# First expert's rows by TensorE products instead of a gather, and spare products before and after the expert loops

## What is computed

```python
def hier_moe(x, ...):                       # x is rms_norm(x, norm_ffn)
    # router: best of 4 groups, then the best two of its 8 experts
    ...
    # every expert e, on the rows routed to it:
    hid = jax.nn.silu(xb @ w_gate[e]) * (xb @ w_up[e])     # 1024 -> 512
    return hid @ w_down[e]                                 # 512 -> 1024
    # weighted, and added to the token's row
```

## Time and profile before

| | |
|---|---|
| median of 3 runs | 1993.37 us (1992.31 to 1996.8) |
| the profiled execution | 1999.4 us, its span 1997.7 us |
| TensorE busy | 86% of the span, mean granted clock 0.906 of full speed |
| VectorE, ScalarE, GpSimd busy | 29%, 20%, 12% |
| DMA, share of 16 engines over the span | 57.9% (SyncE's queue), 8.3% (GpSimd's) |
| expert stage of layer 0, rank products to last down product | 612.5 to 1140.8 us |
| expert stage of layer 1 begins | 1442.6 us |

### The profile page before, as it was taken

How to read it: one execution, slowest core, us unless ns; L and a number is a source line. 1 busy time by engine, 2 the same in 40 slices (tenths; PEclk the granted TensorE clock), 3 DMA queues, 4 the chain that set the end, 5 groups by cost and what they waited for, 6 DMA issues and landing times.

```text
span 1997.7 us, 28368 instructions
## 1 busy us (share of the span) xinstructions
PE 1720.3 (86%) x9488; PEld 906.5 (45%) x9489; DVE 575.2 (29%) x1537; ACT 406.3 (20%) x866; POOL 249.2 (12%) x350
## 2 busy tenths in 40 slices
PE   6798998888994889889998789999778898988985
PEld 4455565555452444444443344456434444444332
DVE  2234343333233111111111165663411111111113
ACT  2122223323111111111111123432111111111112
POOL 1132001332001111111111120000011111111110
PEclk9899889989995899998998889997879989999988
DMA  4343103645246999999999770030399999999983
GB/s 146 79 137 96 47 4 109 209 159 172 83 160 271 393 409 405 410 409 408 402 411 405 302 287 1 17 129 1 134 378 410 416 413 410 407 406 404 401 356 142
DMA packets 83610, 516.31 MB, mean 258 GB/s; under 512 B 22746, under 2 KB 41131, under 8 KB 57067
## 3 DMA queue, kind: packets, MB, share of 16 engines
q1 hardware_dynamic: 61962, 461.35, 57.9%
q0 software_dynamic: 21568, 53.93, 8.3%
HBM read 508.03 MB, written 26.52 MB: 268 GB/s over the span
## 4 chain that ended last, share of the span: by engine, by line
PE 70%; DMA 12%; issue 8%; DVE 5%; ACT 3%; SPq 1%; DVEq 1%; ACTq 0%; POOLq 0%; POOL 0%
PE ps L1866 61%; PE ps L1871 9%; DMA mem<-in_moe_w_up 6%; DMA mem<-in_cache_mla 2%; DMA mem<-moe_rows_back 1%; DVE mem L1525 1%; DMA mem<-moe_rows_in,mem 1%; DMA mem<-in_x_sample 1%; SPq L441 1%; ACT mem L936 1%; ACT mem L724 0%; DVE mem L1644 0%; DMA moe_rows_back<-mem 0%; DVE mem L1570 0%; DVE mem L1249 0%
## 5 line engine op out<-in xcount | busy, mean ns | idle before, releaser
L1866 PE MATMUL ps<-mem 128*64 128x512 f32 (+16 forms) x7352 | 1450.7, 494 | 119.7 <-issue 48.6
L1866 PEld LDWEIGHTS ps<-mem 128*64 128x64 f32 (+4 forms) x7352 | 653.3, 153 | 830.7 <-issue 731.5
L1871 PE MATMUL ps<-mem 128*128 128x128 f32 (+3 forms) x2136 | 309.6, 287 | 150.3 <-DVE mem L1525 45.7
L724 ACT ACTIVATE mem<-ps 128x512 f32<-128x512 f32 (+4 forms) x364 | 195.8, 551 | 900.1 <-PE ps L1866 543.9
L1871 PEld LDWEIGHTS ps<-mem 128*128 128x128 f32 (+3 forms) x2136 | 260.1, 169 | 252.0 <-issue 189.4
L1525 DVE TENSOR_TENSOR mem<-mem,ps 64x512 f32<-64x512 f32 x64 | 44.2, 690 | 470.8 <-ACT mem L936 470.8
L653 POOL DMA_INDIRECT mem<-moe_rows_in,mem x70 | 65.3, 933 | 561.4 <-issue 537.6
L1536 DVE COPY mem<-ps 64x512 f32<-64x512 f32 x64 | 44.4, 693 | 313.5 <-PE ps L1866 313.5
L663 POOL DMA_INDIRECT moe_rows_back<-mem x64 | 59.0, 922 | 356.0 <-DVE mem L1536 348.9
L936 ACT ACT_TABLE_LOAD x32 | 41.1, 1283 | 219.5 <-PE ps L1866 219.5
L936 ACT ACTIVATE mem<-ps 64x512 f32<-64x512 f32 x64 | 37.6, 588 | 199.6 <-PE ps L1866 199.2
(11 more groups left out here) (221 smaller groups left out, 501.0 us busy)
## 6 DMA issues: line engine op xcount, KB each, us to landing
mem<-in_moe_w_gate SPq DMA_DIRECT2D x64, 2048.0 KB
mem<-in_moe_w_up SPq DMA_DIRECT2D x64, 2048.0 KB
mem<-in_moe_w_down SPq DMA_DIRECT2D x64, 2048.0 KB, 21.1
mem<-in_cache_mla POOLq DMA_DIRECT2D x160, 160.0 KB, 4.0
mem<-in_cache_mla SPq DMA_DIRECT2D x96, 160.0 KB, 5.0
mem<-moe_rows_back SPq DMA_DIRECT2D x8, 1024.0 KB, 8.9
mem<-in_mla_wo SPq DMA_DIRECT2D x1, 4096.0 KB, 13.2
moe_rows_in<-mem POOLq DMA_DIRECT2D x8, 512.0 KB, 3.5
```

What stands on the lines that cost most here:

```text
L724: return act.activation(out, in_, ACT.Copy)
L1866: return pe.matmul(out, lhsT, rhs, start=start, stop=stop)
L1871: return pe.transpose(out, in_, ident[at:at + n, at:at + n])
```

## The change

The first expert's rows are no longer gathered. VectorE multiplies expert 0's marks with `rstd` into `direct` (128 x 5 x 64), TensorE computes the transposed rows as x (stationary, 128x128) times `direct` (moving, 64 columns), 8 column groups of x by 5 tiles, and VectorE copies them out of PSUM times the norm's gain, in place of ScalarE's `rows_T(0, 0)`. These 40 products go in three pieces between `numbers(1, 1)`, `pre_mm`, `listrow_mm` and `numbers(2, 0)`. GpSimd gathers from expert 1 on, and the two gathers ahead of the loop no longer wait for a transpose. SyncE issues expert 1's gate and up before its wait for the stored rows; only down waits for them, and expert 2's loads wait for `sel_ready` in layer 1 alone. TensorE also runs `keep_busy`: products of the identity with 512 columns of constants, whose result nobody reads, 20 of them in each layer between the last `logits` and the wait for `sel_ready`, and 24 between the end of layer 0's experts and `hidden(0)`.

```diff
-INTO = ((FETCHES + 1) // 2, FETCHES // 2)
+INTO = ((FETCHES + 1) // 2 - 1, FETCHES // 2)
...
+        direct = mem[:, router.at:router.at + TILES * BLK].rearrange("p (t r) -> p t r", t=TILES)
...
@@ SyncE, experts(L)
+                gate_up(1, 0)
                 for b in range(2):
                     sp.wait_ge(sig[f"xn_out{b}"], landed(f"xn_out{b}", SAVES[b] * (L + 1)))
-                gate_up(1, 0)
                 down(1, 0)
-                sp.wait_ge(sig["sel_ready"], happened("sel_ready", L + 1))
                 if L:
+                    sp.wait_ge(sig["sel_ready"], happened("sel_ready", L + 1))
                     sp.wait_ge(sig["state_out"], landed("state_out", 2))
                 gate_up(2, 1)
@@ GpSimd
-                    g.wait_ge(sig["xt_mm"], happened("xt_mm", (NE + 1) * L + q - 1))
-                    turnstile(g)
+                    if not isinstance(q, int) or q > 2:
+                        g.wait_ge(sig["xt_mm"], happened("xt_mm", (NE + 1) * L + q - 1))
+                        turnstile(g)
...
-                for q in range(LOOK):
+                for q in range(1, LOOK):
                     fetch(q, q % 2)
@@ ScalarE
-                rows_T(0, 0)
@@ VectorE
                     mark(q, q % 2)
-                    if q:
+                    if q == 0:
+                        v.drain()
+                        v.tensor_tensor(direct, onehot[0], rstd[:, 0:TILES].unsqueeze(2).broadcast_to([P, TILES, BLK]), ALU.mult
+                                        ).then_inc(sig["direct_ready"], 1)
+                    else:
                         numbers(q - 1, (q - 1) % 2)
...
+                v.wait_ge(sig["xt_mm"], happened("xt_mm", (NE + 1) * L + 1))
+                v.tensor_tensor(xeT[0], ps[:, 5, :].rearrange("p (k t) -> p k t", k=KD),
+                                gainT_ffn[:, L].unsqueeze(2).broadcast_to([P, KD, BLK]), ALU.mult).then_inc(sig["xeT_ready"], 1)
                 numbers(LOOK - 1, (LOOK - 1) % 2)
@@ TensorE
+            def keep_busy(n):
+
+                for _ in range(n):
+                    mm(ps[:, 7, :], ident, mem[:, TILES * D:TILES * D + FF], True, True)
+
             def experts(L):
...
+                pe.wait_ge(sig["lg_ready"], happened("lg_ready", TILES * L + PT))
+                keep_busy(20)
                 pe.wait_ge(sig["sel_ready"], happened("sel_ready", L + 1))
...
+                def first_rows(k0, k1):
+
+                    for k in range(k0, k1):
+                        for T in range(TILES):
+                            last = mm(ps[:, 5, k * BLK:(k + 1) * BLK], x[:, T * D + k:(T + 1) * D:KD], direct[:, T, :],
+                                      T == 0, T == TILES - 1)
+                    if k1 == KD:
+                        last.then_inc(sig["xt_mm"], 1)
...
                 numbers(1, 1)
+                pe.wait_ge(sig["direct_ready"], happened("direct_ready", L + 1))
+                first_rows(0, 3)
 
                 pe.wait_ge(sig["nb_ready"], happened("nb_ready", L + 1))
                 mm(...).then_inc(sig["pre_mm"], 1)
+                first_rows(3, 6)
                 pe.wait_ge(sig["list_ready"], happened("list_ready", L + 1))
...
+                first_rows(6, KD)
                 pe.wait_ge(sig["lst_ready"], happened("lst_ready", L + 1))
-                fetched_T(0, 0, even + 1)
                 numbers(2, 0)
...
             experts(0)
+            keep_busy(24)
```

More of the change, by code:

```diff
@@ L101 @@
     "sum_mm": ("s_mm", UNITS + 23),
+    "direct_ready": ("a_ms", TILES),
     "third_pages0": ("w_a_in", 1),
@@ L2229, in expert @@
                     last.then_inc(sig["gu_mm"], 1)
-                    fetched_T(e + 1, 1 - b, (odd if b == 0 else even + 1) + pair + 1)
+                    fetched_T(e + 1, 1 - b, (odd if b == 0 else even) + pair + 1)
                     numbers(e + LOOK, 1 - b)
```

## The result

The changed kernel takes 2022.94 us in the median of 3 runs (2018.4 to 2028.85) against 1993.37 us: a ratio of 1.0147, with a 95% interval of 1.010 to 1.0193. It is slower by 1.5%, some 29 us. The forecast was slower by 13.0 us, and its range ended at 2014 us. The profiled execution lasted 2018.4 us, with a span of 2016.7.

The account below looks back on a forecast made before the run. Work ahead of the end of expert 0's gate and up was taken to set each layer's end; +1.8, +4.0 and +7.2 made +13.0 us, from 1993.4 to 2006.4 us, range 1996 to 2014.

Parts of the forecast that it names:

- What bounds the kernel: Expert loops: products and weight loads start from expert 0's gate and up; each microsecond ahead comes out at layer end.
- absorbed by transfers: Rival in the expert loops: if loads set the end, waits swallow the delays and 0 to 4 us remain; chance 0.04.
- The price of a spare product: Ahead of rank products: 0.43 us a record, 17.2 us per 20, plus 1.7 for a clock fall; gaps too short.
- The rival that they fit: Spare products in their gaps: at 0.22 us a record they end in time, about -10 us, 1983; chance 0.13.
- Between the layers: Before layer 1's first projection: 24 spare products delay by 8.2 us, the clock gives back 4, leaving +4.0 us.
- Rank products to the end of numbers 1: Start of each expert stage: 7.0 us, between 6.5 and 8, against 7.5 before.
- The first rows: Expert 0's rows in each layer: 80 records at the logits' 0.122 us, 9.8 us; 11.1 by the transposes.
- Gate and up: Expert 0's products after the first rows: as long as before, with the clock low again.
- The sum by stage: Whole kernel: +1.8 us in layer 0, +4.0 between the layers, +7.2 in layer 1, +13.0 in all.
- The clock stays high: Rival, from spare products into gate and up: high clock gives time back, total +6 to +9 us; chance 0.09.
- A stall in the new code: Rival in TensorE's new stretch: one pause like GpSimd's unexplained 8.47 us, total +21 us, 2015; chance 0.04.
- SyncE's earlier loads: Weights of experts 1 and 2 land some 5 us earlier, worth nothing because expert 3's load waits for expert 0.

Follow-up runs that it names:

- e9: e7 without its 12 spare products between the layers: 1976.29 us, ratio 0.9923 against the kernel before.
- e2: The kernel before with only the 20, 20 and 24 spare products added: 2011.15 us, ratio 1.0112.
- e3: The changed kernel with neighbouring columns of x, not every eighth, as the first rows' stationary operand: 2025.7 us in a single execution.
- e5: The changed kernel with the edits of e3 and e4 together: 2024.11 us in a single execution.
- e4: The changed kernel with two more spare products after each of the first seven column groups of the first rows: 2049.11 us in a single execution.
- e8: The kernel before with only 10, 10 and 12 spare products added: 1986.94 us, ratio 0.9988.
- e1: The changed kernel without any spare products: 2004.02 us, ratio 1.0062 against the kernel before.
- e7: e6 with 10, 10 and 12 spare products: 1978.64 us, ratio 0.9942 against the kernel before.
- e10: The changed kernel without its 24 spare products between the layers: 2017.7 us, ratio 1.0128 against the kernel before.
- e6: The changed kernel without spare products, first rows with marks stationary and x moving 512 columns at a time: 1981.69 us, ratio 0.9961 against the kernel before.

## Why the prediction was right and wrong

- **What bounds the kernel.** Right. Each microsecond ahead of expert 3's load came out at the end of the layer: the loop took 492.4 us before and after in layer 0, and 491.6 and 492.3 in layer 1. Nothing was absorbed by transfers in the changed kernel, and exchanging the operands moved the same point the other way.
- **The price of a spare product.** Right. 48 records took 20.87 us, 0.43 each, as the earlier trace rows said. From the last logits to the rank products lie 18.7 us in either layer (1432.89 + 22.37 less 1.76 for the rank products, as in e9, less 1434.84, where the logits end), forecast 18.9. The fall of the clock within them came too, 0.50 over 595.31 to 597.31, and cost about 1.5 us for the 1.7 taken. The rival that they fit is out; e2, which has nothing else, is slower by 1.1%.
- **Between the layers.** Right, +4.8 for +4.0. The first spare product came 2.26 us after the last down product, not 1.5.
- **Rank products to the end of numbers 1.** 5.2 us (613.0 to 618.2) for the 7.0 that I took, below the bound of 6.5: the high clock gave back more than the 1 us I allowed.
- **The first rows: the step that failed.** I priced 80 records at 0.122 us by the logits, 9.8 us, with 11.1 by the transposes as the upper bound. They took 638.7 - 618.2 less 0.26 and 0.78 for the small products between them, 19.5 us, 0.24 each, and the same in layer 1. The excess is 9.7 us in each layer. That is why even the forecast's sum of all its high bounds, +21 us, fell short: it had 11.1 us for this term. The forecast took a record of the right kind and didn't ask about two things in which it differed. The logits ran at clock 1.00 with a stationary operand of neighbouring columns; the first rows run at 0.50, which I had foreseen for gate and up right behind them, and not applied here. And their stationary operand has every eighth column, which the diff shows (`:KD`). The earlier trace rows held a warning: 8 transposes of 128x128 at the low clock took 1.95 us, 0.244 each, nearly double the 0.139 that stood as the upper bound (this came from transposes of 64 rows, also at 0.50). e3 to e5 show that the step alone costs the whole 0.12 us, and the low clock alone 0.08 to 0.095 of it.
- **Gate and up.** Forecast at 9.6 and 8.6 us as before; about 10.1 and 9.5 after, 0.5 and 0.9 more. The clock was at 0.50 when they began, as forecast.
- **The sum by stage.** Layer 0: -0.2 (spares), -1.8, +9.7 (first rows), +0.5 for the rest make +8.0 with rounding, the difference between +9.8 and the forecast +1.8. Layer 1: +15.9 for +7.2. Between the layers +0.8. Of the 30.5 us the forecast lacked 17.5. The one term, twice, is 19.4; the quicker rank products and numbers give some 3 back, and gate and up and the stage between the layers add the rest.
- **The clock stays high** (rival). It didn't, and by e4 it wouldn't have helped the loads of every eighth column.
- **A stall in the new code** (rival). There was none on TensorE; GpSimd's unexplained 8.38 us before its first gather is still there, now beneath the first rows.
- **SyncE's earlier loads.** Costed at nothing, and nothing was seen of them; they weren't tried alone.

## What to carry to other kernels

When a product is priced by a row of its kind, compare the operand's step and the granted clock too, and look at who is busy: with the 64 moving columns of this case the weight load is the price, and the wide operand should move and the narrow one be stationary (20 records instead of 80 here, and -8 us instead of +12). Filler work ahead of a wait must end within the gap, or what stands behind it on the engine is late: measure one piece, with a fall of the clock in it, and stay below the gap. Here even fitting filler gave no gain that the times can tell (e8, 0.9988). When two causes each suffice to make something slow, removing them one at a time shows little of either; try both together.

## What the runs showed of the hardware

- A weight load of an fp32 product with 128 columns took 0.12 us at clock 1.00 for neighbouring columns and for every second one, 0.24 for every fourth and every eighth. At clock 0.50 it took 0.20 to 0.215 for neighbouring columns and 0.22 to 0.24 for every eighth.
- Transposes whose input has the same step of eight columns didn't pay for it at the high clock: 1.05 us for 8 of 128x128 in the changed kernel between the layers, 0.13 each. At 0.50 such a transpose took 0.244 us, and one of 64 rows 0.139. Why a product pays and a transpose doesn't stays open.
- A spare product's record, 0.43 us at clock 1.00, took 0.85 at 0.50, in e4. Behind 17 us of spare products the clock fell again as soon as the first rows began: 0.86 over 615 to 620 us, 0.50 from 620 on.
- TensorE's first spare product comes 2.15 to 2.26 us after the last down product of the loop, with nothing that the profile shows to wait for.
- Between the layers a VectorE operation of 128x16 values took 5.03, 2.09, 4.82, 4.74 and 4.63 us in five profiles (before, e1, e7, e9, e10), where a GpSimd addition of 128x1024 values ran beside it, and 0.17 or 0.18 us in the ten others, where none did.
- The part of the program ahead of the first expert stage varied between 589 and 612 us with kernels that don't differ there, and single executions of the kernel before between 1979 and 2003. A difference of 0.4% was told with 8 runs of e6 and 24 of the kernel before; one of 0.12% (e8) wasn't, with 12 and 24.
